# Stage boundaries of a ten-stage transformer kernel: token halves, a diagonal product for the norm, a two-scalar tile pass

## The chip, the cores and the metric

The kernel runs on one core of one Trainium2 chip. The metric is the device time of one execution in microseconds; the median of three runs is given. Engines are named TensorE (PE in the rows), its weight load (PEld), VectorE (DVE), ScalarE (ACT), GpSimd (POOL) and SyncE (SP), which issues the loads of the weights.

## What is computed

Two transformer layers and a third block work on x of 256 tokens by 1024 features in fp32. Each has the same frame, cut here to what the boundaries compute:

```python
h = rms_norm(x, norm_w) * (1.0 + scale) + shift        # scale, shift, gate: columns of c @ mod_w
y = mixer_ab(h) or mixer_cd(h) or swiglu(h)             # swiglu: (silu(h @ g) * (h @ u)) @ w_out
x = x + gate * rms_norm(y, norm_w2)                     # first two layers
x = x + 0.5 * g1 * swiglu(h); x = x + g2 * (y_mix @ w_out)   # third block: y is not normed
return rms_norm(x, final_norm)
```

rms_norm divides a row by the root of its mean square plus 1e-6.

## The kernel before, in words

**Stages.** The order is ab (projections and attention), its output product abo, f0 (swiglu), cd and its output cdo, f1, f2 (swiglu), in2 (convolution and state space, with glu), its output o2, f3 (swiglu), end. A boundary lies between the last products of one stage and the first of the next: abo to f0, f0 to cd, cdo to f1, f1 to f2, f2 to in2, o2 to f3, f3 to end.

**Split products.** Every fp32 weight half (128 x 1024) is split by ScalarE into a rounded part HI (L961) and by VectorE into the rest LO (L1371); activations likewise into HH and HLo. A product is three matmuls (mm3, L462; rows, L507). All matmuls stand on line 413, all ScalarE operations on line 952.

**Weights.** A plan (L37) lists the chunks of 1 MB in their order: w chunks with two halves each, and mod chunks, which VectorE reduces into two columns of scale, shift or gate (L1361). weave mixes mod chunks among the w chunks of a stage. SyncE loads them into 5 buffers (L2075). HI and LO are rings of 6 slots: the split of w half number s waits until TensorE has marked half s-6 as used (L960). Walk (L134) decides at which point of each engine's program a split is issued, by program order alone: `use` and `weight` go ahead by up to four halves. Every engine works its program in order.

**swiglu stage** (TensorE L556, ScalarE L1052, VectorE L1516). Step j of 22 makes 128 hidden features: 48 matmuls with 256 columns into one bank, Silu, product and split into HDH and HDL (buffers j mod 3), then the down step j-2: 12 matmuls of 512 columns into PSUM banks 0 to 3. Banks 0 and 1 hold token half 0, banks 2 and 3 token half 1. Down step 19 runs with step 21; steps 20 and 21 run last, both for half 0, then both for half 1. On ScalarE and VectorE the last act of the stage is `use((tag, "dn", 10), 0, 3)` and its twin (L1079, L1543): they issue the next stage's splits that the ring allows, the first being the second half of the next stage's first chunk, whose slot belongs to down step 19.

**Boundary.** With a normed y (f0, cd, f1, f2 as targets): ScalarE squares each bank of y with a row sum (L1033), VectorE multiplies it by the gate row (L1463), the root comes from logarithm and exponential on ScalarE and one Newton step on VectorE (L1398), and the residual is added in one pass of 1024 columns per half (L1479). Where y is not normed (in2, f3, end), add_gated (L1499) does it without root. Then modulate: TensorE turns x by transposes (L549) per half, between blocks of fill products whose result is not read (busy_wide, 8, 4 and 4 or 4, 0 and 4); ScalarE squares the rows of both halves, one root is made for both, VectorE writes it into a diagonal (L1420), TensorE spreads it over all partitions with a product against minus ones (L553), ScalarE copies it out (L994); then per tile k of 8: VectorE multiplies the turned x by the scale column and the spread root (L1436), ScalarE adds the shift and rounds (L1003), VectorE makes the rest (L1431). The first product of the next stage needs tile 0. In the attention outputs (out_half, L643) each of 8 steps is marked used behind its product for the second half.

**The end** (L1966 to L1971, L2076): root and final gain per half, one write of 512 KB for each.

## Time and profile before

| | us |
|---|---|
| runs, median (lowest to highest) | 1244.28 (1243.93 to 1245.1) |
| the profiled execution, its own time | 1245.95 |
| its span | 1244.1 |
| TensorE busy | 1150.2 |
| VectorE busy | 933.0 |
| ScalarE busy | 584.8 |

The busy times are sums over the span; a share of an engine is an average over stages that have different limits. Times in the rows count from the span's start. A matmul of 512 columns is shown as 0.39 us long but the next starts 0.23 behind it, since they are pipelined.

### The profile page before, as it was taken

What the parts mean: (1) busy time and instruction counts of PE and PEld (TensorE: products, weight loads), DVE (VectorE), ACT (ScalarE), POOL (GpSimd) and SP (SyncE); (2) the same over time, 40 slices, a digit from 0 to 9 for tenths busy, and PEclk for the clock granted to TensorE, in tenths of its full rate; (3) what the DMA queues carried; (4) which work ended last, traced back from release to release, by engine and by line L of the source; (5) the groups of instructions that cost most, each with busy time, mean ns of one, the idle gap of its engine ahead of it and who ended that gap; (6) DMA issues with size and microseconds to landing.
All of it is one profiled execution on the core that took longest, in us unless ns stands there. A gap on an engine that the chain in (4) does not pass through costs nothing.

```text
span 1244.1 us, 19935 instructions
## 1 busy us (share of the span) xinstructions
PE 1150.2 (92%) x8342; PEld 1046.7 (84%) x8342; DVE 933.0 (75%) x1630; ACT 584.8 (47%) x960; POOL 74.5 (6%) x106
## 2 busy tenths in 40 slices
PE   2697898999998998899999999999989979999996
PEld 1695578999997996799999889999979967999996
DVE  5888858888776966788888688887666867765545
ACT  1434755443455457634444554444443355444433
POOL 1000000000000000186000000000000000000000
PEclk8799899999998998999999999999989999999999
DMA  9993234788982951477798447789622542765730
GB/s 374 360 381 139 117 136 179 305 328 280 336 317 100 379 213 41 148 288 263 310 261 333 184 178 289 284 245 353 263 107 97 109 178 101 265 249 193 180 131 34
DMA packets 40809, 280.75 MB, mean 226 GB/s; under 512 B 4736, under 2 KB 5264, under 8 KB 7952
## 3 DMA queue, kind: packets, MB, share of 16 engines
q1 hardware_dynamic: 37296, 269.27, 59.3%
q0 software_dynamic: 2416, 7.92, 2.1%
q10 hardware_dynamic: 1008, 2.30, 0.5%
q8 instruction: 65, 1.06, 0.3%
q14 instruction: 24, 0.20, 0.1%
HBM read 277.85 MB, written 1.10 MB: 224 GB/s over the span
## 4 chain that ended last, share of the span: by engine, by line
PE 68%; DVE 19%; DMA 6%; ACT 6%; issue 1%; ACTq 0%; SPq 0%; DVEq 0%
PE PS L413 68%; DMA raw<-WS 6%; DVE LO L1371 5%; DVE raw L1361 4%; ACT HI L952 2%; DVE TMP L1471 1%; DVE SC L1575 1%; ACT SQ L952 1%; DVE TMP L1436 1%; ACT HH L952 1%; ACT SC L952 1%; DVE SC L1560 1%; DVE HLo L1431 0%; PE PS L617 0%; DVE RS L1575 0%
## 5 line engine op out<-in xcount | busy, mean ns | idle before, releaser
L413 PE MATMUL PS<-HH,HI 128*128 128x256 f32 x1748 | 502.3, 287 | 27.7 <-ACT HH L952 24.9
L413 PE MATMUL PS<-HLo,HI 128*128 128x256 f32 x1748 | 503.9, 288 | 0.2
L413 PE MATMUL PS<-HH,LO 128*128 128x256 f32 x1748 | 500.5, 286 | 0.0
L1371 DVE TENSOR_TENSOR LO<-raw,HI 128x1024 fp32r<-128x1024 f32 x340 | 403.9, 1226 | 106.0 <-ACT HI L952 105.9
L952 ACT ACTIVATE HI<-raw 128x1024 fp32r<-128x1024 f32 x340 | 339.6, 1048 | 96.5 <-PE PS L413 58.7
L413 PEld LDWEIGHTS PS<-HH,HI 128*128 128x128 f32 x1748 | 341.2, 195 | 36.0 <-DVE LO L1371 20.5
L413 PEld LDWEIGHTS PS<-HH,LO 128*128 128x128 f32 x1748 | 341.1, 195 | 2.9
L413 PEld LDWEIGHTS PS<-HLo,HI 128*128 128x128 f32 x1748 | 340.5, 195 | 2.8 <-DVE HLo L1431 1.6
L1361 DVE CUSTOM_DVE_ANT_0 raw<-raw,CB,SM 128x1024 f32<-128x1024 f32 x168 | 210.6, 1285 | 23.1 <-DMA raw<-WS 23.0
L413 PE MATMUL PS<-HI,HDH 128*128 128x512 f32 x352 | 140.2, 398 | 0.0
L413 PE MATMUL PS<-HI,HDL 128*128 128x512 f32 x352 | 139.5, 396 | 0.0
L413 PE MATMUL PS<-LO,HDH 128*128 128x512 f32 x352 | 138.9, 394 | 0.0
L952 ACT ACTIVATE HDH<-FB 128x256 fp32r<-128x256 f32 x88 | 36.8, 418 | 205.6 <-DVE FB L1532 205.5
L952 ACT ACTIVATE FB<-PS 128x256 f32<-128x256 f32 (+1 forms) x94 | 37.9, 404 | 130.8 <-PE PS L413 130.6
L413 PEld LDWEIGHTS PS<-HI,HDL 128*128 128x128 f32 x352 | 66.4, 189 | 15.9
L413 PEld LDWEIGHTS PS<-LO,HDH 128*128 128x128 f32 x352 | 66.5, 189 | 12.8
L413 PEld LDWEIGHTS PS<-HI,HDH 128*128 128x128 f32 x352 | 66.4, 189 | 12.4
L1532 DVE TENSOR_TENSOR FB<-FB,PS 128x256 f32<-128x256 f32 x88 | 36.6, 416 | 52.0 <-ACT FB L952 51.9
L1535 DVE TENSOR_TENSOR HDL<-FB,HDH 128x256 fp32r<-128x256 f32 x88 | 37.7, 429 | 45.9 <-ACT HDH L952 45.9
L413 PE MATMUL PS<-HI,HH 128*128 128x512 f32 (+2 forms) x176 | 61.3, 349 | 7.0 <-DVE HLo L1453 5.8
L952 ACT ACTIVATE SC<-PS 128x512 f32<-128x512 f32 (+3 forms) x57 | 31.5, 569 | 75.8 <-PE PS L413 53.4
L413 PE MATMUL PS<-LO,HH 128*128 128x512 f32 (+2 forms) x176 | 60.2, 342 | 0.0
(235 smaller groups left out, 1008.2 us busy)
## 6 DMA issues: line engine op xcount, KB each, us to landing
raw<-WS SPq DMA_DIRECT2D x255, 1024.0 KB, 5.3
SC<-scratch POOLq DMA_DIRECT2D x2, 1024.0 KB, 16.1
FB<-gates_out POOLq DMA_DIRECT2D x3, 512.0 KB, 5.1
SQ<-gates_out POOLq DMA_DIRECT2D x3, 512.0 KB, 9.6
X<-xT ACTq DMA_DIRECT2D x1, 1024.0 KB, 6.8
SC<-ssm POOLq DMA_DIRECT2D x2, 512.0 KB, 4.3
out<-TMP SPq DMA_DIRECT2D x2, 512.0 KB, 2.6
CB<-vecs SPq DMA_DIRECT2D x1, 512.0 KB, 6.5
```

The lines of the kernel that those rows point to most:

```text
L413: return e.matmul(o, l, r, start=start, stop=stop, skip_group_check=True)
L952: return e.activation(o, a, f, **k)
L1361: e.tensor_tensor_reduce(x, x, CB[:, :], 1.0, S("mb")[:, c:c + 1], O.mult, O.add, MV[:, c:c + 1]) \
L1371: e.tensor_tensor(LO[:, s % HL, :], raw_half(j, h), HI[:, s % HL, :].bitcast(fp32), O.subtract).then_inc(*D.up(("lo", s)))
L1436: e.scalar_tensor_tensor(TMP[:, k, :], turned(k), AV[:, k:k + 1], RS[:, 3, :], O.mult, O.mult) \
L1471: e.tensor_tensor(gy[qt][:, c], PS[:, b, :], grow(tag)[:, c], O.mult).then_inc(*D.up(("gy", tag, b)))
L1532: e.tensor_tensor(HF[:, j % 2, :], SIL[:, j % 2, :], bank((key, 0))[:, 256:512], O.mult) \
L1535: e.tensor_tensor(HDL[:, j % 3, :], HF[:, j % 2, :], HDH[:, j % 3, :].bitcast(fp32), O.subtract) \
L1560: e.tensor_scalar(s3[:, n, :], s3[:, n, :], gg[:, n:n + 1], None, O.mult) \
L1575: e.tensor_tensor_reduce(s3[:, n, :], bank(("s", tag, i))[:, n * kw:(n + 1) * kw], reverse(BI[:, bh + h0 + n, 0:kw]), 1.0, sk[:, n:n + 1] ...
```

## The change

Last down steps: 19 leaves the loop; steps 19, 20 and 21 run together, token half 0 first (both banks per step), then half 1 bank by bank, and each is marked used behind its product for the last bank. out_half does the same with its last two steps in the last half. Squares and row sums are scaled by 1/32 and summed by halves of 512 columns; each token half has its own root, whose Newton step takes two operations and leaves a factor of -2 in the root (gates and diagonals carry -0.5). The residual is added by halves of 512. TensorE turns x by a product with the diagonal of roots, so that turning and scaling are one product; there is no spread root. All fill stands ahead of it in one block of 20 or 12. A tile is then one VectorE pass with two scalars (scale and shift), a rounding copy and a subtraction. The fourth split of the next weights moves behind the tiles on VectorE; behind the roots on ScalarE. In f1, f2 and f3 the plan puts no mod chunk into the first four entries. Turned tiles 0 and 1 lie in bank 0, 2 and 3 in bank 1 and so on. GV takes -0.5 as a factor where y is normed.

The diff, cut (TensorE first, then ScalarE, then VectorE and the end; "..." also stands for removed lines, which the listing above has):

```diff
-    def weave(main, extra, tail=5):
+    def weave(main, extra, tail=5, head=0):
         out, e = [], list(extra)
         for i, x in enumerate(main):
             out.append(x)
-            want = min(len(extra), (i + 1) * len(extra) // (len(main) - tail))
+            want = min(len(extra), max(0, i + 1 - head) * len(extra) // (len(main) - tail - head))
             while len(extra) - len(e) < want:
...
-    plan += weave(ffn("f1"), mods(24, 8))
-    plan += weave(ffn("f2"), mods(32, 8))
+    plan += weave(ffn("f1"), mods(24, 8), 5, 4)
+    plan += weave(ffn("f2"), mods(32, 8), 5, 4)
...
-    plan += weave(ffn("f3"), mods(40, 2), 20)
+    plan += weave(ffn("f3"), mods(40, 2), 16, 4)
...
-            def modulate(tag, sc, fill=(0, 0, 0)):
+            def modulate(tag, sc, fill=0):
                 mods(sc + 8)
+                busy_wide(fill)
                 for qt in range(2):
-                    busy_wide(fill[qt])
...
+                    w.wait_ge(*D.at(("dg", tag, qt)))
                     for k in range(8):
-                        e.transpose(turned(k)[:, qt * 128:qt * 128 + 128], X[:, qt, k * 128:k * 128 + 128], C("ident"))
...
+                        i = mm(turned(k)[:, qt * 128:qt * 128 + 128], X[:, qt, k * 128:k * 128 + 128], dg[:, qt, :],
+                               qt == 0 and k % 2 == 0, True)
+                        if qt and k % 2:
+                            i.then_inc(*P.up(("turned", tag, k - 1), ("turned", tag, k)))
...
-                    if j > 1:
+                    if 1 < j < 21:
                         down(j - 2)
-                key = (tag, "dn", 10)
...
+                wts = {j: weight((tag, "dn", j // 2), j % 2) for j in (19, 20, 21)}
+                def last_down(j, qt, h, done):
+                    w.wait_ge(*D.at(("hdl", tag, j)))
+                    rows(tag, (HDH, HDL), j % 3, wts[j], False, j == 21,
+                         [("down", tag, j), used((tag, "dn", j // 2), j % 2)] if done else [], (qt,), (h,))
+                for j in (19, 20, 21):
+                    for h in range(2):
+                        last_down(j, 0, h, False)
+                for h in range(2):
+                    for j in (19, 20, 21):
+                        last_down(j, 1, h, h == 1)
...
+                ends = ks[-1] == 7 and qt == gives
+                for k in ks[:-2] if ends else ks:
+                    wt = half_ready(k)
+                    rows(name, (HH, HLo), k, wt, k == begins, k == 7, [used((name, k // 2), k % 2)] if qt == gives else [],
                          (qt,))
+                if ends:
+                    wts = [half_ready(k) for k in ks[-2:]]
+                    for h in range(2):
+                        for k, wt in zip(ks[-2:], wts):
+                            rows(name, (HH, HLo), k, wt, k == begins, k == 7,
+                                 [used((name, k // 2), k % 2)] if h else [], (qt,), (h,))
...
-            def row_sums(tag, qt, ready):
+            def row_sums(tag, qt):
                 w.wait_ge(*A.now())
-                w.wait_ge(*ready)
...
+                for h in range(2):
+                    c = slice(h * 512, h * 512 + 512)
+                    w.wait_ge(*(XIN.at("in") if tag == "ab" else D.at(("x", tag, qt, h))))
+                    fn(junk(tag, qt)[:, c], X[:, qt, c], F.Square, scale=1.0 / 32,
+                       accum_out=x_[:, 2 * qt + h:2 * qt + h + 1]).then_inc(*A.up(("s", tag, qt, h)))
+            def first_root(tag, qt, parts_):
                 w.wait_ge(*A.now())
-                w.wait_ge(*G.at("consts"))
-                fn(z_[:, c], s_[:, c], F.Ln, bias=eps[:, 0:1], scale=1.0 / 1024).then_inc(*A.up())
+                w.wait_ge(*D.at(("v0", tag, qt)))
+                fn(z_[:, qt:qt + 1], parts_[:, 2 * qt + 1:2 * qt + 2], F.Ln, bias=v0_[:, qt:qt + 1]).then_inc(*A.up())
                 w.wait_ge(*A.now())
-                fn(r_n[:, c], z_[:, c], F.Exp, scale=-0.5).then_inc(*A.up(("rexp", tag, q)))
+                fn(r_n[:, qt:qt + 1], z_[:, qt:qt + 1], F.Exp, scale=-0.5).then_inc(*A.up(("rexp", tag, qt)))
             def roots(tag):
                 for qt in range(2):
-                    row_sums(tag, qt, XIN.at("in") if tag == "ab" else D.at(("x", tag, qt)))
...
+                    row_sums(tag, qt)
+                    first_root(tag, qt, x_)
             def modulate(tag, sh, sc):
                 high(walk.mods(sc + 8))
                 if tag != "ab":
                     next_weights(tag, 4)
-                    roots(tag)
                 for k in range(8):
                     w.wait_ge(*D.at(("tmp", tag, k)))
-                    fn(HH[:, k, :], TMP[:, k, :], F.Identity, bias=MV[:, sh + k:sh + k + 1]) \
-                        .then_inc(*A.up(("hh", tag, k)))
+                    fn(HH[:, k, :], TMP[:, k, :], F.Copy).then_inc(*A.up(("hh", tag, k)))
...
+            def bank_square(tag, name, b):
+                w.wait_ge(*P.at(("acc", name, b)))
+                fn(junk(tag, b // 2)[:, b % 2 * 512:b % 2 * 512 + 512], PS[:, b, :], F.Square, scale=1.0 / 32,
+                   accum_out=h_[:, b:b + 1]).then_inc(*A.up(("s", tag + "y", b // 2, b % 2)))
+            def add_normed(tag, name, early):
                 w.wait_ge(*A.now())
-                for b in (2 * qt, 2 * qt + 1):
...
+                bank_square(tag, name, 0)
+                bank_square(tag, name, 1)
+                first_root(tag + "y", 0, h_)
+                if early:
+                    next_weights(tag, 3)
+                bank_square(tag, name, 2)
+                row_sums(tag, 0)
+                bank_square(tag, name, 3)
+                first_root(tag + "y", 1, h_)
+                first_root(tag, 0, x_)
+                row_sums(tag, 1)
+                first_root(tag, 1, x_)
...
+            def mean(tag, qt, parts_):
+                a, b = [parts_[:, 2 * qt + h:2 * qt + h + 1] for h in range(2)]
+                w.wait_ge(*A.at(("s", tag, qt, 0)))
+                e.tensor_scalar(v0_[:, qt:qt + 1], a, 1e-6, None, O.add).then_inc(*D.up(("v0", tag, qt)))
+                w.wait_ge(*A.at(("s", tag, qt, 1)))
+                w.wait_ge(*D.now())
+                e.tensor_tensor(v_[:, qt:qt + 1], v0_[:, qt:qt + 1], b, O.add).then_inc(*D.up())
+            def row_root(tag, qt):
+                v, q, r = [x[:, qt:qt + 1] for x in (v_, q_, r_n)]
+                w.wait_ge(*A.at(("rexp", tag, qt)))
+                w.wait_ge(*D.now())
+                e.tensor_scalar(q, v, r, r, O.mult, O.mult).then_inc(*D.up())
+                w.wait_ge(*D.now())
+                e.scalar_tensor_tensor(r, q, -3.0, r, O.add, O.mult).then_inc(*D.up())
+                w.wait_ge(*D.now())
...
+            def spread(tag, qt):
+                row_root(tag, qt)
+                w.wait_ge(*CONST.at("in"))
+                e.tensor_scalar(dg[:, qt, :], C("ident"), r_n[:, qt:qt + 1], -0.5, O.mult, O.mult) \
+                    .then_inc(*D.up(("dg", tag, qt)))
             def roots(tag):
-                mean(tag, 2)
-                row_root(tag, 2)
-                w.wait_ge(*CONST.at("in"))
                 for qt in range(2):
-                    e.tensor_scalar(dg[:, qt, :], C("ident"), r_n[:, qt:qt + 1], -1.0, O.mult, O.mult) \
-                        .then_inc(*D.up(("dg", tag)))
+                    mean(tag, qt, x_)
+                    spread(tag, qt)
...
             def modulate(tag, sh):
-                if tag != "ab":
-                    next_weights(tag, 4)
-                    roots(tag)
                 w.wait_ge(*D.now())
                 def rest(k):
                     w.wait_ge(*A.at(("hh", tag, k)))
-                    e.scalar_tensor_tensor(HLo[:, k, :], TMP[:, k, :], MV[:, sh + k:sh + k + 1],
-                                           HH[:, k, :].bitcast(fp32), O.add, O.subtract).then_inc(*D.up(("hlo", tag, k)))
+                    e.tensor_tensor(HLo[:, k, :], TMP[:, k, :], HH[:, k, :].bitcast(fp32), O.subtract) \
+                        .then_inc(*D.up(("hlo", tag, k)))
                 for k in range(8):
-                    w.wait_ge(*A.at(("free", ("rb", tag))))
-                    e.scalar_tensor_tensor(TMP[:, k, :], turned(k), AV[:, k:k + 1], RS[:, 3, :], O.mult, O.mult) \
+                    w.wait_ge(*P.at(("turned", tag, k)))
+                    e.tensor_scalar(TMP[:, k, :], turned(k), AV[:, k:k + 1], MV[:, sh + k:sh + k + 1], O.mult, O.add) \
                         .then_inc(*D.up(("tmp", tag, k)))
                     if tag == "ab" and k == 1:
                         low(walk.catch_up(walk.unit - 1, 1))
                     if k:
+                        w.wait_ge(*D.at(("tmp", tag, k - 1)))
                         rest(k - 1)
+                w.wait_ge(*D.at(("tmp", tag, 7)))
                 rest(7)
+                if tag != "ab":
+                    next_weights(tag, 4)
...
+            def gated_bank(tag, name, b, normed):
                 w.wait_ge(*ROWIN.at(("grow", tag)))
-                for b in (2 * qt, 2 * qt + 1):
...
+                w.wait_ge(*P.at(("acc", name, b)))
+                if normed:
+                    w.wait_ge(*A.at(("s", tag + "y", b // 2, b % 2)))
+                c = slice(b % 2 * 512, b % 2 * 512 + 512)
+                e.tensor_tensor(gy[b // 2][:, c], PS[:, b, :], grow(tag)[:, c], O.mult).then_inc(*D.up(("gy", tag, b)))
             def new_rows(tag, qt):
-                e.scalar_tensor_tensor(X[:, qt, :], gy[qt], r_n[:, qt:qt + 1], X[:, qt, :], O.mult, O.add) \
-                    .then_inc(*D.up(("x", tag, qt)))
+                for h in range(2):
+                    c = slice(h * 512, h * 512 + 512)
+                    e.scalar_tensor_tensor(X[:, qt, c], gy[qt][:, c], r_n[:, qt:qt + 1], X[:, qt, c], O.mult, O.add) \
+                        .then_inc(*D.up(("x", tag, qt, h)))
             def add_normed(tag, name, sc, gain, early):
-                factors(sc, gain)
-                gated_rows(tag, name, 0, True)
-                own_norm(tag, 0)
+                factors(tag, sc, gain)
+                gated_bank(tag, name, 0, True)
+                gated_bank(tag, name, 1, True)
+                mean(tag + "y", 0, h_)
                 row_root(tag + "y", 0)
+                new_rows(tag, 0)
                 if early:
-                    new_rows(tag, 0)
                     next_weights(tag, 3)
-                gated_rows(tag, name, 1, True)
...
+                gated_bank(tag, name, 2, True)
+                gated_bank(tag, name, 3, True)
+                mean(tag, 0, x_)
+                mean(tag + "y", 1, h_)
                 row_root(tag + "y", 1)
                 new_rows(tag, 1)
+                spread(tag, 0)
+                mean(tag, 1, x_)
+                spread(tag, 1)
             def add_gated(tag, name):
                 for qt in range(2):
-                    gated_rows(tag, name, qt, False)
-                    w.wait_ge(*D.now())
-                    e.tensor_tensor(X[:, qt, :], X[:, qt, :], gy[qt], O.add).then_inc(*D.up(("x", tag, qt)))
+                    for h in range(2):
+                        c = slice(h * 512, h * 512 + 512)
+                        gated_bank(tag, name, 2 * qt + h, False)
+                        w.wait_ge(*D.now())
+                        e.tensor_tensor(X[:, qt, c], X[:, qt, c], gy[qt][:, c], O.add).then_inc(*D.up(("x", tag, qt, h)))
+                        if (qt, h) == (1, 0) and tag != "end":
+                            mean(tag, 0, x_)
                     if tag == "f3" and qt == 0:
                         next_weights(tag, 3)
+                if tag != "end":
+                    spread(tag, 0)
+                    mean(tag, 1, x_)
+                    spread(tag, 1)
...
-                e.scalar_tensor_tensor(gy[qt], X[:, qt, :], r_n[:, qt:qt + 1], SC[:, 1024:2048], O.mult, O.mult) \
-                    .then_inc(*D.up(("result", qt)))
+                e.tensor_scalar(r_n[:, qt:qt + 1], r_n[:, qt:qt + 1], -0.5, None, O.mult).then_inc(*D.up())
+                w.wait_ge(*D.now())
+                for h in range(2):
+                    c = slice(h * 512, h * 512 + 512)
+                    e.scalar_tensor_tensor(gy[qt][:, c], X[:, qt, c], r_n[:, qt:qt + 1], SC[:, 1024 + h * 512:1536 + h * 512],
+                                           O.mult, O.mult).then_inc(*D.up(("result", qt, h)))
...
-                w.wait_ge(*D.at(("result", qt)))
-                e.dma_start(out[:, qt, :], gy[qt]).then_inc(*OUT.up("all", by=16))
+                for h in range(2):
+                    c = slice(h * 512, h * 512 + 512)
+                    w.wait_ge(*D.at(("result", qt, h)))
+                    e.dma_start(out[:, qt, c], gy[qt][:, c]).then_inc(*OUT.up("all", by=16))
```

In the programs of ScalarE and VectorE the calls follow: roots("in2") and next_weights("f3", 3) with roots("f3") stand ahead of modulate on ScalarE; add_normed is called once per boundary. The swiglu stage of ScalarE and of VectorE (L1052, L1516) is not edited.

## Rows read from the trace of the kernel before

**Rows 1.** The page, busy time: share of the span, instructions.

```profile
PE 1150.2 (92%) x8342; PEld 1046.7 (84%) x8342; DVE 933.0 (75%) x1630; ACT 584.8 (47%) x960; POOL 74.5 (6%) x106
```

**Rows 2.** Windows f0 and f0 to cd: us, busy us by engine, granted clock, DMA share, GB/s.

```profile
193.00:385.40 192.40, 190.61 (x1320) 177.66 (x1321) 159.37 (x272) 86.99 (x128) 1.46 (x2) 0.99 0.76 285
385.40:396.30 10.90, 6.68 (x35) 4.61 (x33) 8.09 (x21) 6.52 (x17) 0.00 (x0) 1.00 0.36 132
```

**Rows 3.** The chain that ended last: start us, length us, what.

```profile
316.25 13.47 DMA raw<-WS
...
722.74 185.78 PE PS L413 x1357
```

**Rows 4.** Order of time, f1 to f2: start, length, operation, [idle before <- releaser].

```profile
702.86 0.39 PE L413 MATMUL PS<-HI,HDH 128*128 128x512 f32 x1
...
705.21 0.42 DVE L1535 TENSOR_TENSOR HDL<-FB,HDH 128x256 fp32r<-128x256 f32 x1 [1.31 <-ACT HDH L952]
...
705.86 2.01 ACT L952 ACTIVATE HI<-raw 128x1024 fp32r<-128x1024 f32 x2 [0.69 <-PE PS L413]
...
706.96 2.36 DVE L1371 TENSOR_TENSOR LO<-raw,HI 128x1024 fp32r<-128x1024 f32 x2 [1.33 <-ACT HI L952]
...
709.46 1.29 DVE L1471 TENSOR_TENSOR TMP<-PS,SC 128x512 f32<-128x512 f32 x2
...
711.29 1.98 PE L413 MATMUL PS<-HH 128*128 128x512 f32 x8
...
711.41 0.16 DVE L1403 TENSOR_TENSOR NR<-NR 128x1 f32<-128x1 f32 x1 [0.41 <-ACT NR L952]
...
722.22 0.39 PE L413 MATMUL PS<-HH,HI 128*128 128x256 f32 x1 [1.61 <-ACT HH L952]
```

**Rows 5.** VectorE's groups by form: busy us, mean ns, idle before.

```profile
L1436 DVE SCALAR_TENSOR_TENSOR TMP<-PS,AV,RS 128x256 f32<-128x256 f32 x56 | 26.2, 479 | 7.8 <-ACT RS L952 7.7
...
L1909 DVE TENSOR_SCALAR TMP<-PS,SM 128x256 f32<-128x256 f32 x4 | 1.9, 480 | 0.1
...
L1453 DVE TENSOR_TENSOR HLo<-TMP,HH 128x256 fp32r<-128x256 f32 x4 | 1.7, 426 | 1.9 <-ACT HH L952 1.9
...
L1407 DVE SCALAR_TENSOR_TENSOR NR<-NR 128x1 f32<-128x1 f32 x10 | 1.6, 159 | 0.3
```

**Rows 6.** Windows from E to the next stage: cdo to f1, f2 to in2, o2 to f3.

```profile
507.79:517.45 9.66, 6.51 (x36) 4.63 (x34) 6.46 (x18) 6.08 (x16) 0.53 (x1) 1.00 0.63 228
...
913.97:922.40 8.43, 4.86 (x27) 3.22 (x26) 6.29 (x14) 3.74 (x9) 0.00 (x0) 0.97 0.45 178
1037.13:1044.56 7.43, 4.82 (x28) 3.23 (x26) 5.28 (x13) 2.60 (x7) 0.53 (x1) 1.00 0.50 149
```

**Rows 7.** Order of time, the end of the kernel.

```profile
1239.73 1.28 DVE L1970 SCALAR_TENSOR_TENSOR TMP<-X,NR,SC 128x1024 f32<-128x1024 f32 x1
```

**Rows 8.** The page, DMA issues: count, KB each, us to landing.

```profile
out<-TMP SPq DMA_DIRECT2D x2, 512.0 KB, 2.6
```

**Rows 9.** Windows of one step (8.76 us) of f1, the fullest of VectorE.

```profile
570.56:579.32 8.76, 8.76 (x64) 8.22 (x64) 8.24 (x9) 3.95 (x7) 8.18 (x8) 1.00 0.67 239
```

**Rows 10.** Windows near the start of f1, f2, f3: the granted clock is PEclk, third last.

```profile
520.00:522.00 2.00, 2.00 (x11) 2.00 (x11) 2.00 (x6) 1.44 (x3) 0.00 (x0) 0.50 0.00 0
724.00:726.00 2.00, 2.00 (x12) 2.00 (x11) 2.00 (x6) 1.43 (x3) 0.00 (x0) 0.50 0.00 0
1046.00:1048.00 2.00, 2.00 (x11) 2.00 (x11) 2.00 (x6) 1.20 (x3) 0.00 (x0) 0.50 0.01 4
```

**Rows 11.** Order of time, the first tiles of f2.

```profile
724.18 0.48 DVE L1436 SCALAR_TENSOR_TENSOR TMP<-PS,AV,RS 128x256 f32<-128x256 f32 x1
...
724.71 0.41 PE L413 MATMUL PS<-HLo,HI 128*128 128x256 f32 x1
...
724.97 0.48 DVE L1436 SCALAR_TENSOR_TENSOR TMP<-PS,AV,RS 128x256 f32<-128x256 f32 x1
...
725.35 0.41 PE L413 MATMUL PS<-HLo,HI 128*128 128x256 f32 x1
```

135 lines of the change are left out of this document (37 added, 98 removed).

## The prediction

> **What bounds the kernel now.** I read the page first: TensorE is busy for 92% of the span [rows 1]. That alone says little, because the share mixes ten stages, so I cut the span at the places where TensorE pauses. Inside a stage it hardly pauses: in f0 it is busy 190.6 of 192.4 us. Between two stages it does: of the 10.9 us between f0 and cd it has work for 6.7, part of which is fill whose result nobody reads [rows 2]. The chain of waits confirms it. Through f2 it is one piece of TensorE, 185.8 us; f0 alone is different, its chain goes through VectorE and a DMA piece of 13.5 us at 316 us [rows 3]. So a microsecond saved or lost at a boundary is a microsecond of the kernel, except at the boundary into f0, where VectorE and its loads set the end anyway.
>
> Last I read the boundary f1 to f2 in order of time [rows 4]. Call E the start of the fill behind the last real product, 711.29. The first of the last 36 products starts at 702.86, the last 0.23 before E: 0.234 us each. The reader should see four things: ScalarE's HI split at 705.86 waited for TensorE (24 products before the end are 5.6 us; the wait ended 5.4 before E); by the code the squares of y come behind that pair of splits; VectorE's gate product at 709.46 comes directly behind its own pair of LO splits; and from it to f2's first product at 722.22 are 12.8 us. VectorE's pair is what starts the boundary, and a TensorE slot release starts the pair.
>
> **The slot that is released later.** The weights of the next stage need ring slots. There are six, and split number s waits for the products of unit s-6. The second half of the next stage's first tile therefore waits for the down step 19. Before, that step is complete 24 products before the end. In the change steps 19, 20 and 21 are run by half: all of token half 0 (18 products), then half 1 by bank, and step 19 is marked used only in the last bank, when 30 of 36 products are done. That is 6 x 0.234 = 1.4 before E, 4.2 us later. ScalarE and VectorE still issue this split ahead of everything of the boundary: on ScalarE the squares of both token halves, the roots and row sums are queued behind it, on VectorE the gate products, and TensorE waits for these. So what ends early on TensorE (bank 0 now 21 products before the end, 4.9 us) is not looked at until the splits are over. This holds behind f0, f1 and f2; behind f3 no weights follow, and behind abo, cdo and o2 the slots wait for steps that are released as before.
>
> **f1 to f2, in time from E.** Wait over at -1.2, HI pair to +0.85, LO pair (1.1 behind, 2.36 long [rows 4]) to +2.3, first gate product +2.4 instead of -1.8. From there on VectorE carries: four half gate products and four half residual passes, 0.65 each, 5.2; fourteen one-column operations on the path at 0.2 from start to start (0.16 busy, 0.03 idle before each [rows 5]), 2.8; two diagonals at 0.25, 0.5; three waits for ScalarE's logarithm and exponential, 0.4 each as before [rows 4], and one of 0.8 for the square of bank 3, which now stands behind the row sums of half 0, 2.0; the turn of the last half, first tile, its rounding and TensorE's start, 1.5; small gaps 0.4. Together 12.4 where before were 12.8: the shorter chain (no broadcast product, no copy of it) is nearly eaten by operations cut in two. First product at +14.8 instead of +10.9: **+3.8**.
>
> **f0 to cd** has the same order and the same 10.9 before [rows 2]: +3.8. Here the projections take three products a tile instead of six, so VectorE's pace through the eight tiles counts: two passes, 0.79 from tile to tile [rows 11]. A scalar pass from PSUM is no cheaper than the three-operand pass, 480 against 479 ns; the plain subtraction, 426, is cheaper than the rest with the shift, which is a three-operand pass too [rows 5]: 0.05 on seven tiles, -0.3. **+3.5**.
>
> **f2 to in2** has no norm of y. Before, 8.4 from E (913.97) to the first product [rows 6]. After: LO pair to +2.3; four gate products and four additions 5.2, small ones before the first diagonal 1.2, that diagonal and the last half's root 1.6, tail 1.5: +11.6. +3.2, less 0.3 of tile pace: **+2.9**.
>
> **cdo to f1.** No slot is late. 9.7 before [rows 6]. The order on ScalarE is now square of bank 2, two half row sums, square of bank 3, which ends at +1.4 instead of +0.9; then VectorE's last gate product, four small ones, root, residual to +5.0, diagonal 0 at +5.7, the root of half 1 and its diagonal at +7.0, first product +8.6: **-1.0**.
>
> **abo to f0** is the same, but f0's chain is VectorE's [rows 3]. There the tile loop ends 1.3 earlier, and the LO split that stood ahead of it (1.2) now stands behind it: **0.0**.
>
> **o2 to f3.** 7.4 before [rows 6]; HI waits for a step released as before. Bank 2 ends three products earlier, the residual goes by halves, half 0 has its root early: gate product and addition of bank 3 end at +1.9, diagonals at +2.6 and +4.1, first product +5.4: **-2.0**.
>
> **The end.** Half 0's earlier end buys nothing, because its root waits on VectorE behind the last addition; the last result is ready at 1241.2 instead of 1241.0 [rows 7], but the last write is half as large: 0.5 MB took 2.6 us to landing [rows 8], and I take 0.6 off for half of it (my guess between 0 and half of 2.6): **-0.4**. **The start**: tile pace -0.3; there VectorE waits for loads, so I give the added small operations nothing; if the loads do not cover them, eight at 0.2 are +1.6.
>
> **The plan.** In f1 and f2 no modulation chunk comes in the first four entries, then one per 1.5 entries instead of 1.75: two reductions of 1.2 per step instead of 1.7, +0.34 us per step. VectorE's fullest window of one step holds 8.24 of 8.76 us [rows 9], so 8.6: hidden by TensorE, 0; if it spills, 0.1 in each of 16 steps of two stages, up to +3. HDL of step 21 is ready at 705.63 and now wanted after 12 products, 705.67 [rows 4]: 0, or 0.1 at four places. The products of the last steps are as many as before; their order costs nothing.
>
> **Sum**: -0.3 + 0 + 3.5 - 1.0 + 3.8 + 2.9 - 2.0 - 0.4 = +6.5 us. The profiled execution took 1245.95 (span 1244.1), which gives 1252.5; it lies 1.7 over the median of the runs, 1244.28, so the forecast of the median is **1250.8**. About 0.2% (2.5 us) is what a measurement tells from no change.
>
> **The clock.** After every boundary TensorE falls from 2.4 to 1.2 GHz: granted 0.50 near the start of f1, f2 and f3 [rows 10], after pauses of 1 to 2 us between bits of fill (f2's first product waited 1.6 [rows 4]). Three products then take 0.64, so a tile of f with six takes 1.3 us where VectorE needs 0.79 [rows 11]. Now the fill is one block of 20 (4.4 us), then a pause. With the late slot that pause is over 7 us: low as before, and f2 may stay low longer, up to +1.7. Into f1 and f3 the pause is 1 to 2 us, about as before: 0, or -1.7 each. The Trainium skill ("TensorE: Matmul & The Clock Gate", Part 1, What's actually happening) says that "the default state is throttled, and activity releases the throttle"; by that rule the denser fill could hold the clock, and the sum would be +3.1. The trace so far shows the fall behind every fill.
>
> **Rivals.**
> 1. *The clock stays at 2.4 GHz into f1 and f3*: 1250.8 - 3.4 = 1247.4. For it: fewer and shorter pauses there. Against: it fell at both before [rows 10]. Chance 0.12.
> 2. *The slot wait costs nothing* (faster). Place: ScalarE's HI split behind f0, f1 and f2. If its release were not what holds VectorE's pair, these three would be -0.7, -0.4 and -1.4 instead of +10.2 together: 6.5 - 12.7 = -6.2, 1238.1. Each microsecond of wait counts three times; below 2.1 at each the change wins. For it: nothing else got longer. Against: before, the same wait ends just as step 19 does, and the gate product stands directly behind the pair. Chance 0.13.
> 3. *The late slot is paid in part, the gains balance it*: 1244.3. It needs waits near 2 us at three places. Chance 0.05.
> 4. *VectorE or HDL becomes the bound in f1, f2*: 1250.8 + 3 = 1253.8. Chance 0.08.
> The forecast itself has 0.62, with 1247.5 to 1254 as its own range. That the turned and scaled product does not shorten the chain is already in it: 0.4 at f1 to f2.
>
> **Numbers.** Range 1244 to 1256: down to rival 3, past rival 1; up to rival 4 with the longer low clock of f2. Only rival 2 and a little above lie outside. Faster by over 0.2%: rival 2, 0.13. Within: 0.07. Slower: 0.80.
>
> **What would show it.** Right: behind f0, f1, f2 ScalarE waits for TensorE until 1.2 before the last product, HI and LO pairs follow, then the squares; TensorE idles for some 7 us behind its fill; distances from E near 14.8, 14.8, 11.6 and 8.6, 8.6, 5.4. Wrong: squares of bank 0 about 4.5 before E; a granted clock of 1.00 through f1's first 4 us; VectorE over 8.7 in a step.

## The result, and the profile after

The changed kernel takes **1265.62 us** (median of 4 runs, 1264.75 to 1271.66) where the kernel before takes 1244.69 beside it: ratio 1.0173, interval 1.0153 to 1.0192. It is slower, as forecast, but by 20.9 us instead of 6.5, and outside the range. The profiled execution is the longest of the four, 1271.66 (span 1269.9; the other spans are 1262.9 to 1264.1). Its surplus of some 6 us is not in the boundaries: stage f1 takes 198.7 us in it, 193.8 before, with one wait of TensorE for a LO split at 673.59 of 3.50 us; in three runs that differ from it in the boundaries alone (a2, a3 and a4 below) f1 takes 194.4 to 195.5. So I compare boundaries, and take whole times from the medians.

The gap from the fill (E) to the next stage's first product, us, before and after, with what the forecast said:

| into | before | after | forecast of the growth | measured |
|---|---|---|---|---|
| f0 | 9.66 | 9.77 | 0.0 | +0.1 |
| cd | 10.93 | 18.25 | +3.5 | +7.3 |
| f1 | 9.66 | 9.77 | -1.0 | +0.1 |
| f2 | 10.93 | 18.44 | +3.8 | +7.5 |
| in2 | 8.43 | 14.51 | +2.9 | +6.1 |
| f3 | 7.43 | 6.53 | -2.0 | -0.9 |

Together +20.2, close to the 20.9 of the result. The forecasts for cd and in2 contain 0.3 that was to be gained inside the stage. Between the boundaries the profiled pair differs, apart from f1, by +1.5 us in f0, +1.0 in in2, -0.8 in cd and -0.9 in f2. The boundary f1 to f2 of the changed kernel in order of time, the one that answers to [rows 4] (start, length, operation, idle before and what released it):

```profile
723.33 2.01 ACT L958 ACTIVATE HI<-raw 128x1024 fp32r<-128x1024 f32 x2 [5.02 <-PE PS L412]
724.42 2.36 DVE L1382 TENSOR_TENSOR LO<-raw,HI 128x1024 fp32r<-128x1024 f32 x2 [5.65 <-ACT HI L958]
724.53 4.73 PE L412 MATMUL PS<-HH 128*128 128x512 f32 x20
725.37 0.60 ACT L958 ACTIVATE SQ<-PS 128x512 f32<-128x512 f32 x1
726.92 1.29 DVE L1488 TENSOR_TENSOR TMP<-PS,SC 128x512 f32<-128x512 f32 x2
734.74 1.41 DVE L1493 SCALAR_TENSOR_TENSOR X<-TMP,NR,X 128x512 f32<-128x512 f32 x2
736.76 0.29 DVE L1430 TENSOR_SCALAR RS<-CN,NR 128x128 f32<-128x128 f32 x1
737.10 6.11 PE L412 MATMUL PS<-RS,X 128*128 128x128 f32 x32 [7.84 <-DVE NR L1407]
738.27 0.29 DVE L1430 TENSOR_SCALAR RS<-CN,NR 128x128 f32<-128x128 f32 x1
741.85 0.99 DVE L1449 TENSOR_SCALAR TMP<-PS,AV,MV 128x256 f32<-128x256 f32 x2 [3.30 <-PE PS L412]
742.43 0.87 ACT L958 ACTIVATE HH<-TMP 128x256 fp32r<-128x256 f32 x2 [3.75 <-DVE TMP L1449]
```

The reader should see three things. The HI pair starts 1.2 us before E (724.53), the gate product 2.4 behind it: the late slot does what was forecast, to a tenth. The turned product is 32 passes (a pass is one record of the trace), where the code has 16 products, and takes 6.11 us. And VectorE's first tile stands 3.30 us waiting for it. The first product starts at 742.97.

The page's group for the turn in the changed kernel, and then in the kernel before (busy us, mean ns, idle before):

```profile
L412 PE MATMUL PS<-RS,X 128*128 128x128 f32 x224 | 34.9, 329 | 36.6 <-DVE NR L1407 36.6
```

```profile
L549 PE MATMUL PS<-CN,X 128*128 128x128 f32 x112 | 16.6, 299 | 6.2 <-DVE X L1480 4.5 <-DVE TMP L1471 1.0 <-DMA CN<-consts 0.6
```

112 transposes in seven boundaries have become 224 passes of 112 products, and the idle time before them has gone from 6.2 to 36.6 us, all of it put down to VectorE's root. It is a sum over seven turns: 7.91, 7.84 and 6.12 behind f0, f1 and f2, 1.4 each into f0 and f1, none into f3, and 11.9 at the start of the kernel, where nothing is lost by it (the first product of ab starts at 40.59, before at 40.65).

The granted clock (third last column) in the changed kernel, at the start of f1, during the turn into f2 and at the start of f2 and f3, which answers to [rows 10]:

```profile
core 0: us, PE busy (x) PEld busy (x) DVE busy (x) ACT busy (x) POOL busy (x), PEclk, DMA share, GB/s
526.00:528.00 2.00, 1.97 (x16) 1.72 (x15) 2.00 (x6) 1.07 (x3) 0.00 (x0) 1.00 0.00 0
737.00:739.00 2.00, 1.90 (x9) 1.90 (x10) 0.98 (x6) 1.44 (x3) 0.00 (x0) 0.50 0.00 0
739.00:741.00 2.00, 2.00 (x11) 2.00 (x11) 0.00 (x0) 0.00 (x0) 0.00 (x0) 0.50 0.00 0
744.00:746.00 2.00, 1.98 (x16) 1.75 (x14) 1.88 (x6) 1.12 (x3) 0.00 (x0) 1.00 0.00 0
1070.00:1072.00 2.00, 1.98 (x16) 1.75 (x15) 1.90 (x6) 1.25 (x3) 0.00 (x0) 1.00 0.00 0
1072.00:1074.00 2.00, 2.00 (x17) 1.97 (x17) 2.00 (x6) 0.92 (x3) 0.00 (x0) 1.00 0.00 0
```

It is turned round. Behind f0, f1 and f2 the turn runs at 1.2 GHz, behind pauses of 7.91, 7.84 and 6.12 us, until its last 1 to 2 us. But at all six boundaries the next stage's first products run at 2.4 GHz, where before the clock was at 0.50 for 3 to 6 us of each start.

### The profile page after: what moved, and what is told of

Its sections match the earlier page's. It is cut to its first block, busy times and chain, and to the rows that moved or that the text cites. A ratio compares the mean times of both kernels' runs of the same rounds, so it can differ in the third digit from the quotient of the medians.

```text
span 1269.9 us, 20331 instructions
## 1 busy us (share of the span) xinstructions
PE 1165.7 (92%) x8464; PEld 1062.5 (84%) x8464; DVE 940.7 (74%) x1668; ACT 581.8 (46%) x999; POOL 69.7 (5%) x106
## 4 chain that ended last, share of the span: by engine, by line
PE 57%; DVE 28%; DMA 7%; ACT 6%; issue 2%; SPq 0%; DVEq 0%; ACTq 0%
PE PS L412 56%; DVE LO L1382 10%; DVE raw L1372 7%; DMA raw<-WS 7%; ACT HI L958 3%; DVE HLo L1444 1%; DVE FB L1557 1%; DVE SC L1600 1%; DVE TMP L1488 1%; DVE TMP L1716 1%; DVE TMP L1449 1%; ACT HDH L958 1%; ACT SQ L958 1%; PE PS L613 1%; DVE X L1493 1%
## 5 line engine op out<-in xcount | busy, mean ns | idle before, releaser
L412 PE MATMUL PS<-HH,LO 128*128 128x256 f32 x1748 | 495.4, 283 | 0.0
L412 PEld LDWEIGHTS PS<-HH,HI 128*128 128x128 f32 x1748 | 336.0, 192 | 25.7 <-DVE LO L1382 17.3
L412 PEld LDWEIGHTS PS<-HLo,HI 128*128 128x128 f32 x1748 | 335.7, 192 | 7.5 <-DVE HLo L1444 6.7
L412 PEld LDWEIGHTS PS<-HH,LO 128*128 128x128 f32 x1748 | 336.0, 192 | 2.8
L1372 DVE CUSTOM_DVE_ANT_0 raw<-raw,CB,SM 128x1024 f32<-128x1024 f32 x168 | 210.1, 1285 | 18.3 <-DMA raw<-WS 18.2
L1557 DVE TENSOR_TENSOR FB<-FB,PS 128x256 f32<-128x256 f32 x88 | 36.6, 416 | 52.9 <-ACT FB L958 52.8
L412 PE MATMUL PS<-RS,X 128*128 128x128 f32 x224 | 34.9, 329 | 36.6 <-DVE NR L1407 36.6
L412 PEld LDWEIGHTS PS<-RS,X 128*128 128x128 f32 x224 | 33.6, 241 | 40.4 <-DVE NR L1407 27.2
```

What stands on the lines that cost most here:

```text
L412: return e.matmul(o, l, r, start=start, stop=stop, skip_group_check=True)
L1372: e.tensor_tensor_reduce(x, x, CB[:, :], 1.0, S("mb")[:, c:c + 1], O.mult, O.add, MV[:, c:c + 1]) \
L1557: e.tensor_tensor(HF[:, j % 2, :], SIL[:, j % 2, :], bank((key, 0))[:, 256:512], O.mult) \
```

## The experiments

The theory: (a) the late slot costs the boundaries behind f0, f1 and f2 about 4.2 us each; (b) the rest is the turned product, double in passes, behind the root, and at the low clock. Rivals: the plan or VectorE's supply of weights inside the stages; the clock at the stages' starts; the halved passes. Each run had its own runs of the kernel before beside it (median 1245.4 to 1246.8).

| run | edit | median us | ratio to before |
|---|---|---|---|
| a1_slot | changed, step 19 back in the loop | 1251.55 | 1.0058 [1.0043, 1.0073] |
| b1_late | before, with the late slot | 1258.49 | 1.0093 [1.0073, 1.0113] |
| a2_order | changed, other order of passes | 1261.87 | 1.0141 [1.0126, 1.0156] |
| a3_onepass | changed, plain transposes | 1259.47 | 1.0114 [1.0100, 1.0128] |
| a4_fill | changed, long fill | 1261.22 | 1.0133 [1.0119, 1.0148] |
| a5_plan | changed, old transfer order | 1269.51 | 1.0188 [1.0166, 1.0209] |
| a6_slot_plan_order | a1, with the edits of a2 and a5 | 1250.41 | 1.0038 [1.0027, 1.0049] |
| b2_plan | before, new transfer order | 1245.24 | 0.9992 [0.9981, 1.0004] |
| b3_behind | before, turn behind the root | 1273.45 | 1.0217 [1.0196, 1.0238] |
| c1_nw | a1, fourth LO split ahead | 1253.04 | 1.0050 [1.0032, 1.0067] |
| c2_all | a1 + a2 + fill + c1 | 1247.72 | 1.0013 [1.0002, 1.0024] |
| d1_turn_back | a1, turn as before (start late) | 1256.69 | 1.0080 [1.0061, 1.0099] |
| d2_turn_fill | d1 + fill in every pause | 1253.57 | 1.0054 [1.0036, 1.0073] |
| e1_more_fill | before, fill in every pause | 1243.97 | 0.9975 [0.9965, 0.9986] |
| g1_turn_back | d1, start mended | 1251.33 | 1.0042 [1.0025, 1.0060] |
| g2_turn_fill | d2, start mended | 1250.94 | 1.0040 [1.0027, 1.0054] |
| h1_plan_fill | b2 + e1 (7 products in place of 5 in the last fill into in2) | 1244.20 | 0.9991 [0.9979, 1.0003] |
| a8_slot_onepass | a1 + a3 | 1247.63 | 1.0015 [1.0002, 1.0027] |

**The late slot, from both sides.** a1_slot puts step 19 back:

```
-                    if 1 < j < 21:
+                    if j > 1:
                         down(j - 2)
-                wts = {j: weight(...) for j in (19, 20, 21)}
+                wts = {j: weight(...) for j in (20, 21)}
...
-                for j in (19, 20, 21):
+                for j in (20, 21):
```

> The changed kernel, with step 19 of every feed-forward stage put back into the loop: only steps 20 and 21 are split by token half and bank, so step 19's slot is given back before them. Everything else stays changed. Theory (the late slot costs the boundaries behind f0, f1 and f2 about 4.2 us each, since the residual and root operations queue on ScalarE and VectorE behind the HI and LO of the late weight halves): the gaps behind f0, f1 and f2 (18.25, 18.44, 14.51 us from the fill to the first product) fall by about 4 us each, and the whole by about 12 us, to 1253. Rival (those gaps are long because of the turned product and the low clock alone, and the slot wait lies beside other work): the gaps stay within 1 us of what they are, and the time within 3 us of 1265.

b1_late carries the changed kernel's end of `ffn` (steps 19 to 21 by half and bank) into the kernel before, with nothing else:

> The kernel before, with one part of the change: the last three steps of every feed-forward stage (19, 20, 21) are taken by token half and the second half's by bank, so that step 19's slot is given back only after 30 of the stage's last 36 products. Theory (the late slot alone prices the boundaries behind f0, f1 and f2): each of their gaps (10.93, 10.93 and 8.43 us) grows by about 4 us less what the earlier end of the first half gives back, 3 to 4 us each; the whole grows by 8 to 12 us, to 1253 to 1257. Rival (the slot wait costs nothing, the first half that ends early pays for it): within 2 us of 1244.7 or below it.

a1 measured 1251.55, 14.1 less than the changed kernel; its gaps behind f0, f1 and f2 are 13.71, 14.61 and 8.48 (before the edit 18.25, 18.44, 14.51), -14.4 together. b1 measured 1258.49, 12.9 over the kernel before; its gaps are 16.31, 15.28 and 12.80 (10.93, 10.93, 8.43), +14.1. The rows of b1 at f1 to f2, E at 715.53:

```profile
714.32 2.01 ACT L958 ACTIVATE HI<-raw 128x1024 fp32r<-128x1024 f32 x2 [5.02 <-PE PS L413]
715.42 2.36 DVE L1377 TENSOR_TENSOR LO<-raw,HI 128x1024 fp32r<-128x1024 f32 x2 [5.66 <-ACT HI L958]
717.92 1.29 DVE L1477 TENSOR_TENSOR TMP<-PS,SC 128x512 f32<-128x512 f32 x2
```

and of a1, E at 714.04:

```profile
708.62 2.01 ACT L958 ACTIVATE HI<-raw 128x1024 fp32r<-128x1024 f32 x2 [0.69 <-PE PS L412]
709.71 2.36 DVE L1382 TENSOR_TENSOR LO<-raw,HI 128x1024 fp32r<-128x1024 f32 x2 [1.33 <-ACT HI L958]
712.22 1.29 DVE L1488 TENSOR_TENSOR TMP<-PS,SC 128x512 f32<-128x512 f32 x2
722.11 6.78 PE L412 MATMUL PS<-RS,X 128*128 128x128 f32 x32 [3.37 <-DVE NR L1407]
```

With the late slot the HI pair starts at E-1.2 and the gate product at E+2.4; without it at E-5.4 and E-1.8. This is shown: the slot is worth 12 to 14 of the 21 us (by the recorded ratios a1 is 14.3 under the changed kernel, b1 11.6 over the kernel before). The rival, that it costs nothing, is out.

**The turned product.** a3_onepass puts `e.transpose(..., C("ident"))` in place of `mm(..., dg[:, qt, :], ...)`, behind the same waits:

> The changed kernel, with the turned product replaced by a plain transpose against the identity: 16 transposes in one pass each in place of 16 products in two passes each, behind the same waits. It leaves out the scaling of the rows by their roots, and nothing else. Theory (the turn as a product takes twice the passes, 6.11 us at the low clock and 3.84 at the high one): the turn takes about half, tile 0 comes 1.5 to 1.9 us earlier behind f0, f1 and f2 and 1.0 at the other boundaries, the whole falls by 7 to 9 us. Rival (a transpose is no quicker than the product, tile by tile, or the passes are hidden): under 2 us.

It measured 1259.47, -6.2: the mechanism holds, a little under the 7 to 9 expected. All gaps are shorter, behind f0, f1 and f2 by 2.1, 2.3 and 1.9, at the others by 0.6. With the slot put right as well:

> The changed kernel with step 19 back in the loop (1251.6) and, besides, plain transposes in place of the turned products, behind the same waits. It leaves out the scaling of the rows by their roots. Theory (the second pass of each product costs the same with the slot put right): 5 to 6.5 us less, 1245 to 1246.5. Rival (a stage that starts earlier meets a later weight, as the fill showed, so half of it is given back): 1248 to 1249.

1247.63, -3.9, between the two. Its gaps sum to 56.2, less than the 57.0 of the kernel before, and yet its median is 1.9 above; its profiled execution, from which the gaps are read, is one of its fastest, 1245.4. A boundary's microsecond is not always a microsecond of the kernel, as I had taken it; g2 and e1 below show it more clearly. Its turn into f2, at the low clock, and the changed kernel's into f1, at the high one (6.11 at the low one is above):

```profile
719.57 3.67 PE L541 MATMUL PS<-CN,X 128*128 128x128 f32 x16 [3.38 <-DVE NR L1406]
```

```profile
522.20 3.84 PE L412 MATMUL PS<-RS,X 128*128 128x128 f32 x32 [1.42 <-DVE NR L1407]
```

From start to start a pass takes 0.11 us at the granted clock of 1.00 and 0.21 where it is 0.50, transpose and product alike; of the 32 passes in the 6.11 us the first 22 or so run at the low clock, the last ones at the high one. A product has two passes, so it takes twice the time of a transpose.

b3_behind keeps transposes but has TensorE wait for the diagonals first (`w.wait_ge(*D.at(("dg", tag)))` ahead of each half's transposes):

> The kernel before with its 16 transposes of every boundary put behind the diagonals of the roots: TensorE waits for the diagonals first, then transposes, then makes the broadcast product. Nothing else is changed. Theory (what the changed kernel pays in its turned product is that the turn stands behind the root on the path, where before it lay beside VectorE's root): each of the seven boundaries gets 2 us longer at the high clock (16 transposes, 1.09 per 8) and 3 to 4.5 at the low one (2.26 per 16 seen behind f2, less where part overlaps), the whole 14 to 20 us longer, 1259 to 1265. Rival (the turn is hidden by VectorE's tile passes, only its first tile counts): 0.3 to 0.6 us a boundary, under 5 in all.

1273.45, +27.8, more than either theory; but it is not a clean price, as fill went behind the root with the turn. Behind f1:

```profile
735.07 1.97 PE L550 MATMUL PS<-CN,X 128*128 128x128 f32 x8 [6.63 <-DVE RS L1421]
736.69 1.78 PE L413 MATMUL PS<-HH 128*128 128x512 f32 x4
738.31 1.03 PE L550 MATMUL PS<-CN,X 128*128 128x128 f32 x8
739.10 1.17 PE L413 MATMUL PS<-HH 128*128 128x512 f32 x4
740.11 0.59 PE L413 MATMUL PS<-RS,nones 128*128 128x256 f32 x2
```

From the turn's start to the broadcast product are 5.0 us; from start to start the transposes have 1.6 and 0.8 of them, the two pieces of fill 1.6 and 1.0. So half of it is fill, and the turn's place is worth some 2.4 us at a low clock, in a chain of transposes and broadcast product.

a2_order takes the passes as half 0 of tiles 0 to 3, half 1 of tiles 0 to 3, then tiles 4 to 7:

> The changed kernel, with the 32 passes of the turned product in another order: half 0 of tiles 0 to 3, half 1 of tiles 0 to 3, half 0 of tiles 4 to 7, half 1 of tiles 4 to 7, so that tile 0 needs 8 passes of half 0 ahead of its half 1, and no longer 16. Theory (tile 0 waits for TensorE's passes, 0.19 us each at the granted clock of 0.50 and 0.12 at 1.00): behind f0, f1 and f2 tile 0 comes 1.5 us earlier, at the other three inner boundaries 0.4 to 0.9, since there the second diagonal is late; the whole falls by 5 to 7 us. Rival (the first product waits for VectorE's and ScalarE's own queue and not for the passes): no change beyond 1 us.

1261.87, -3.7, but not by the mechanism: the gaps sum to 79.9 instead of 77.3. The first product stands behind all 32 passes in TensorE's order, so no order brings it forward, and the wait for the second diagonal now lies in the middle. Into f0 the clock was low behind that second pause:

```profile
189.74 1.16 PE L412 MATMUL PS<-RS,X 128*128 128x128 f32 x8 [1.41 <-DVE NR L1407]
191.25 4.57 PE L412 MATMUL PS<-RS,X 128*128 128x128 f32 x24 [0.36 <-DVE RS L1430]
```

```profile
192.00:194.00 2.00, 2.00 (x12) 2.00 (x11) 1.52 (x4) 0.83 (x2) 0.00 (x0) 0.50 0.00 0
```

Into f1 the same kernel has the same 8 passes behind a pause of 1.41 us and a second pause of 0.35, and the clock stays at 1.00. So what lowered it into f0 is not shown. Stage f0 gave it back: TensorE's longest wait for LO in it is 1.58 us instead of 2.97, all of them 2.3 instead of 4.2. What else made this kernel faster stays open.

**Place and clock with the slot right.** d1_turn_back is a1 with the turn as before: transposes of the unscaled rows beside VectorE's root, one broadcast product, the three-operand pass. d2_turn_fill adds fill to every pause, five products behind the broadcast among them:

```
-                    for k in range(8):
-                        i = mm(turned(k)[...], X[:, qt, ...], dg[:, qt, :], ...)
+                    for k in range(8):
+                        e.transpose(turned(k)[...], X[:, qt, ...], C("ident"))
+                busy_wide(fill[2])
+                mm(ps[:, 0:256], nones[:, :], RS[:, 2, :], True, True)
+                busy_tail(fill[3])
```

> The changed kernel with step 19 back in the loop (1251.6 us) and the turn made as before: 16 transposes of the unscaled residual while VectorE works out the roots, one product that broadcasts them, the three-operand pass on the tiles. The halved residual passes, the half row sums, the block of fill and the transfer order of the change stay. Theory (with the slot put right, what is left of the loss is the turned product that stands behind the root): behind f0 and f1 the broadcast product waits for the second diagonal at 9.6 us and the first product follows 2.3 us later, 11.9 instead of 13.7 and 14.6; in all 3 to 6 us less, 1246 to 1248, as the kernel before. Rival (the halved passes and added small operations are what is left): within 1.5 us of 1251.6.

> The same kernel as the one with the turn made as before, with fill in every pause of the boundaries: ahead of each turned half, between them, ahead of the broadcast product, and five products behind it (these five read another tile). Theory (the kernel before begins each stage at a granted clock of 0.50 for 3 to 6 us, because TensorE pauses for 1 to 2 us before it; the changed kernel does not): the stages start at 1.00 and the time is 4 to 8 us under that of the same kernel with the block of fill alone, below the kernel before, near 1240. Rival (a stage that starts at the low clock catches up before its supply of weights does, so nothing is gained): within 1.5 us of it.

1256.69 and 1253.57. Both began the fill into f0 3 to 4 us late (185.7 and 185.2, a1 181.7): a fault of the edit in the first stage, so they are run again without it:

> The run with the turn made as before, once more, with a fault of that experiment mended: in the first stage ScalarE copied the broadcast roots only behind three weight splits, so that TensorE's first wait for LO was 15.3 us instead of 10.6 and the fill into f0 began 4 us late (185.7 against 181.7); now it copies them right behind the roots, as the kernel before does. Nothing else differs. Expected by the traces: 4 us less, 1252 to 1253.5, so that to turn behind the root and at the full clock (1251.6) and to turn beside it and start the stages at the low clock cost the same. If the turn beside the root is what should win, 1248 or less.

> The same mending in the kernel with fill in every pause of the boundaries. Expected: 4 us less than 1253.6, 1249 to 1250.5, 2 to 3 under its partner without the fill: what the low clock at the starts of stages costs in all. Above the kernel before (1245) by 4 to 5 us, which then are the halved passes and the added small operations.

1251.33 and 1250.94. So a turn behind the root (a1, 1251.55) and one beside it cost the same. The gaps are not the same: g1's behind f0 and f1 are 12.78 and 12.20 instead of 13.71 and 14.61, others are 0.2 longer, -2.7 in all. What it gains there it loses inside the stages. The low clock at the stages' starts is the near explanation: a1 has the full clock there, and g1 has this into f1:

```profile
518.00:520.00 2.00, 2.00 (x9) 1.91 (x10) 2.00 (x6) 1.11 (x3) 0.00 (x0) 0.50 0.03 8
520.00:522.00 2.00, 2.00 (x15) 2.00 (x14) 2.00 (x6) 1.17 (x4) 0.00 (x0) 0.74 0.00 0
```

But g2 has the full clock at every start (f1 below) and gaps of 57.6 together, 5.3 less than a1, and its median is only 0.4 us under g1, which is not told from nothing. So the clock alone is not where the gain goes:

```profile
522.00:524.00 2.00, 2.00 (x18) 1.96 (x16) 2.00 (x6) 1.17 (x4) 0.00 (x0) 1.00 0.00 0
```

**Fill.** a4_fill has 50 products of fill behind f0 and f1, 36 behind f2:

> The changed kernel, with the fill behind f0 and f1 of 50 products in place of 20 (about 11.7 us in place of 4.7, ending just ahead of the first diagonal at 12.5 us) and behind f2 of 36 in place of 12. Theory (the turned product runs at the granted clock of 0.50 because TensorE was idle for some 8 us before it): the granted clock stays at 1.00 in the turn, its 32 passes take 3.8 us and not 6.1, tile 0 comes about 2 us earlier at these three boundaries, and the whole falls by 5 to 7 us. Rival (the clock falls at these places whatever TensorE does, as it fell in the kernel before): granted clock 0.50 in the turn as before, and no change beyond 1 us, or some loss where the fill ends late.

1261.22, -4.4. The fill bridges the pause and the turn keeps the full clock (boundary f1 to f2):

```profile
717.62 11.53 PE L412 MATMUL PS<-HH 128*128 128x512 f32 x50
730.19 3.84 PE L412 MATMUL PS<-RS,X 128*128 128x128 f32 x32 [1.04 <-DVE NR L1407]
733.85 0.39 PE L412 MATMUL PS<-HH,HI 128*128 128x256 f32 x1
```

3.84 us in place of 6.11, and gaps of 16.31, 16.23 and 12.70, -6.0 together. By the rule that the prediction quoted from the Trainium skill ("TensorE: Matmul & The Clock Gate", Part 1, What's actually happening), activity releases the throttle; this pair of kernels agrees: the same boundary, with and without fill, at 1.00 and 0.50.

e1_more_fill does it to the kernel before:

> The kernel before with more fill in the pauses of its boundaries and nothing else: 7, 5, 6 products in place of 8, 4, 4 into f0 and f1, 15, 4, 7 into cd and f2, 8, 0, 7 in place of 4, 0, 4 into in2, 4, 2, 7 into f3, and five products behind each broadcast product. Theory (the clock, and not the chain of the boundary, is what the kernel before loses at the start of its stages: granted 0.50 to 0.70 for 3 to 6 us at six places, so 1 to 2.5 us each): granted clock 1.00 at the stages' starts and 5 to 10 us less, 1235 to 1240. Rival (VectorE's pace through the tiles, or the weights, hold the start in any case): 0 to 2 us less.

1243.97, 0.25% faster than the runs beside it, far less than expected, though the clock is 1.00 at five of six starts. TensorE then waits longer for its LO splits: in f0 3.9 us in all instead of 1.7. The longest of these waits, 40 us into f0, before and with the fill:

```profile
233.07 0.39 PE L413 MATMUL PS<-HH,HI 128*128 128x256 f32 x1 [0.73 <-DVE LO L1371]
```

```profile
231.88 0.38 PE L413 MATMUL PS<-HH,HI 128*128 128x256 f32 x1 [1.88 <-DVE LO L1380]
```

**The transfer order.** a5_plan takes the changed kernel's order back, b2_plan gives it to the kernel before:

```
-    plan += weave(ffn("f1"), mods(24, 8), 5, 4)
-    plan += weave(ffn("f2"), mods(32, 8), 5, 4)
+    plan += weave(ffn("f1"), mods(24, 8))
+    plan += weave(ffn("f2"), mods(32, 8))
...
-    plan += weave(ffn("f3"), mods(40, 2), 16, 4)
+    plan += weave(ffn("f3"), mods(40, 2), 20)
```

> The changed kernel with the order of the weight transfers of before (modulation halves spread from the first step of f1, f2 and f3, up to five, five and twenty steps from their end). Theory (the plan costs f1 something: 1.5 to 4.8 us by the length of f1 in the profiled run, 198.7 us against 193.8): f1 back to 194 to 195 us, the whole 1 to 4 us lower. Rival (the longer f1 of the profiled run was an accident of that run, and the plan costs nothing or saves something at the stages' starts, where it keeps modulation halves out): within 1 us of 1265, or above it by up to 3.

> The kernel before with the changed order of the weight transfers alone (no modulation half in the first four entries of f1, f2 and f3). Undoing that order in the changed kernel cost 3.9 us. Theory (the new order is worth the same wherever the boundaries stand, since it keeps two reductions of 1.2 us off VectorE while it makes up its arrears at a stage's start): 3 to 4 us faster than before, 1241 to 1242. Rival (it is worth something only in the changed kernel, where the late slot and the late LO split make VectorE late at a stage's start): within 1 us of 1245.

1269.51, 3.9 slower, against the theory; and 1245.24, no difference. Each against the runs of the kernel before beside it, the two are 2 to 3 us apart, and the intervals of their ratios, 1.0153 to 1.0192 and 1.0166 to 1.0209, overlap. So the new order costs the changed kernel nothing and may gain it 2 to 4 us, which is not shown. In the kernel before it gains nothing. h1_plan_fill asks whether it helps the kernel before at the full clock:

> The kernel before with more fill in its pauses (2.9 us faster alone) and with the changed transfer order (0.4 us faster alone, not told from nothing). In the changed kernel that order gave 3.9 us, where the stages start at the full clock and VectorE has arrears. Theory (the order is worth something once TensorE starts the stages at full speed, since then the weights are what it waits for): 1240 to 1242.5, faster than both kernels. Rival (the two do not add): 1243.5 to 1244.5.

1244.20, not told from the kernel before, and not better than e1. With fill like e1's it does not repeat e1's 0.25% either, so I claim no version that is surely faster than the kernel before.

**Together.** a6_slot_plan_order takes back slot and plan, and has the passes in a2's order:

> The changed kernel with three of its costs taken back together: step 19 back in the loop, the transfer order of before, and tile 0's passes ahead. If the three add, as the theory has it: 12 + 2 + 6 us lower, about 1245, the time of the kernel before. If they hide each other (one wait behind the other at the same boundary): between 1248 and 1256.

1250.41; with the single prices as measured (-14.1, -3.7, +3.9) the sum is 1251.7. They add; what was expected wrong is the plan, booked at 2 us of gain, and the order of passes, booked at 6. c1_nw moves VectorE's fourth LO split (`next_weights(tag, 4)`) from behind the tile loop to ahead of it, on top of a1, and c2_all joins the repairs:

> The changed kernel with step 19 back in the loop (the run at 1251.6) and, besides, VectorE's fourth LO split of the next stage's weights put ahead of the tile loop again; the change had moved it behind the tiles. It takes 1.2 us, and VectorE waits there for the turned product in any case, 1.15 us at the high clock and over 3 at the low one. Theory (the split is late behind the tiles, and TensorE's wait for LO at the start of f0, 3.0 us against 0.7 before, comes from it): that wait falls to about 1 us, tile 0 does not come later, 2 to 4 us off the whole, 1248 to 1250. Rival (that wait comes from the loads, not from VectorE's order): within 1 us of 1251.6.

> The changed kernel with every repair found so far: step 19 back in the loop, tile 0's passes ahead, the fourth LO split ahead of the tiles, and fill up to the first diagonal (25 products into f0 and f1, 34 into cd and f2, 19 into in2). The transfer order of the change stays. If they add: 1251.6, less 3.7 (order), less about 2 (fill, over a shorter pause than where it gave 4.4), less 1 to 2 (split) is 1244 to 1245, level with the kernel before. If the order's second pause lowers the clock again (into f0 it did, granted 0.50 from 192 to 195 us), 1247 to 1249.

c1: 1253.04, no gain. TensorE's longest wait for LO in f0 falls from 2.98 to 1.95 us, but a second one of 1.07 comes to it, and in2's first product comes later (gap 10.05 instead of 8.48). c2: 1247.72, 2.1 above the kernel before, inside the band of the second case, but not for its reason: the gap into f0 is 10.33, and f0 starts at the full clock. What the parts gave alone does not add fully.

## Why the prediction was right or wrong

**The slot: right, place and size.** HI at E-1.2, gate product at E+2.4, as written; by itself in the kernel before it lengthens three gaps by 4.4 to 5.4 us each and the whole by 12.9. Rival 2, that it costs nothing, is refuted from both sides.

**The failed step is the tail of the boundary sum**: "the turn of the last half, first tile, its rounding and TensorE's start, 1.5". It measured 4.4 us at f1 to f2, from the second diagonal's end (738.56) to 742.97. The same stretch, from the end of the second diagonal to the first product, at all six boundaries:

| us | into f0, f1, f3 | into cd, f2, in2 |
|---|---|---|
| before (broadcast product and its copy) | 2.37 | 2.37 |
| forecast | 1.3 to 1.6 | 1.5 |
| changed | 2.20 | 4.15, 4.41, 4.01 |
| a4_fill: two passes, clock 1.00 | 2.20 | 2.20 |
| a3_onepass: one pass, clock as granted | 1.65 | 2.10 |

So with one pass at the full clock the term would have been nearly right. Three things were missed in it. The turn is a product now and takes two passes a tile. The passes of half 0 stand ahead of those of half 1, and the first product behind all 32. And after a pause that the same forecast put at "over 7 us" they run at the low clock; each of the last two lines takes one of the causes away, and either brings the term to 2.2 or less. A bound was in reach, from rows of the kernel before at f1 to f2:

```profile
715.02 1.09 PE L549 MATMUL PS<-CN,X 128*128 128x128 f32 x8 [1.75 <-DVE X L1480]
719.37 0.48 DVE L1420 TENSOR_SCALAR RS<-CN,NR 128x128 f32<-128x128 f32 x2
```

Eight transposes took 1.09 us, so 16 behind the roots had to be 2.2 at least from the first diagonal, and twice that at the low clock; I had priced the low clock for the stages' products only. 2.9 of the 3.6 us by which f2's first product came later than forecast are this term (E+18.4 instead of E+14.8), the other 0.7 small operations and waits. Behind f0 and f2 the first product stands at E+18.3 and E+14.5 instead of 14.8 and 11.6, and 2.7 and 2.5 of that are this term; at the full clock, into f0, f1 and f3, it is 1.1 to 1.2 late each, 0.6 to 0.9 of it this term. Against the growth that was forecast these are 13.0 together, and 6.5 + 13.0 = 19.5 stands against 20.9 measured. (In the sum for f2 to in2 the terms as written add to +11.8, not +11.6.)

**Gains that were booked** into f1 (-1.0) and f3 (-2.0) came to +0.1 and -0.9 for the same reason. Into f0 the +0.1 against 0.0 is luck: the first product was expected 8.6 behind E and stands at 9.77, a gain that did not come and had been written off; and TensorE waits for LO in f0 for 4.2 us in all instead of 1.7. The 0.3 for the pace through the tiles, booked at the start, in cd and in in2, did not come either: from tile to tile are 0.77 us before and 0.77 to 0.80 after. The subtraction gains 0.06 (418 against 478 ns), but the scalar pass loses it: it was priced at 480 ns by four operations of another place, and with two column scalars it takes 538:

```profile
L1449 DVE TENSOR_SCALAR TMP<-PS,AV,MV 128x256 f32<-128x256 f32 x56 | 29.6, 538 | 12.9 <-PE PS L412 12.8
```

**The clock: rival 1 came true, and more**: 1.00 at the start of every stage behind a boundary. But it was priced at 1.7 each, and at the starts it is worth far less: 0.4 us for all of them in g2 against g1, 2.9 in e1 against the kernel before. That the next weights hold the start is what e1's longer waits for LO suggest. The clock that counted, that of the turn, was not in the sum.

**The plan** was put at 0, up to +3. It came to 0, or to a gain of 2 to 4 us that the runs do not tell from nothing; no value below nothing was kept.

**The end** was put at -0.4. From the last product (1234.14, now 1259.35) to the span's end are 10.0 us before and 10.5 after, +0.6. The halved writes are no shorter:

```profile
out<-TMP SPq DMA_DIRECT2D x4, 256.0 KB, 2.5
```

where 512 KB took 2.6 [rows 8]: the 0.6 taken off was worth 0.1.

**The balance**: 12 to 14 us are the slot. 4 to 6 are the second pass of the turn and up to 4.4 the low clock in it; these two lie partly in the same time. Put back as a whole, the turn gains nothing (g1 against a1), since at the full clock the new tail, 2.20, is no longer than the old one, 2.37: it was a gain that was booked and did not come. With slot and turn both back (g1) 5.6 us are still left. Its gaps sum to 3.2 more than before, nearly all of it behind f0 and f1, where the second diagonal ends at E+9.9 and E+9.5 instead of E+8.6: up to there the chain of VectorE and ScalarE is 1.0 to 1.3 longer. g1 differs from the kernel before in the halved residual passes and row sums, the roots by half, the order of the last products, the place of the fourth split and of the fill, and the plan. The plan alone costs nothing (b2), and the fourth split put back gained nothing (c1). No run halves the passes alone, so that they are the rest is argued, not shown.

## What to carry to other kernels

When an operation is moved behind the result that it waits for, price it as if nothing hid it: its passes, at the clock that the pause before it leaves, and all that its engine has queued ahead of the first consumer. A buffer released later is paid once for each place where its refill stands ahead of the critical work in an engine's queue, and both a change and its undoing should be run alone to price it. Time gained at a boundary is not always kept: g2 had 5.3 us less in its gaps than a1 and the same time.

## What was not expected of the hardware

- An fp32 product of 128x128 by 128x128 shows two passes (224 records for 112 products), a transpose of the same tile one (112 for 112). From start to start a record takes 0.11 us at the full clock in both, so the product takes twice the time of the transpose. The Trainium skill ("FP8 and Floating Point Precision", TensorE Precision Notes) gives true fp32 four passes. The records here show two; but each of them, with 128 columns, takes nearly as long (0.11 us) as a product of 256 columns in the stages (0.12), so by its time the product agrees with four. Whether a record holds two of them no run shows.
- Pauses of 1.4 us and then 0.4 us around 8 short passes do not settle what the clock is. It stayed at 1.00 in a3_onepass into f0 and in a2_order into f1, and it was at 0.50 behind them in a8_slot_onepass into f0 and in a2_order into f0. With the turn in one piece behind the 1.4 us (changed kernel, f0 and f1) it stayed at 1.00.
- A write of 256 KB takes as long to land as one of 512 KB, 2.5 and 2.6 us.
